# Hybrid decoder trunk: in the state-space mixer, the injection of the next inputs goes behind the state outputs, the direct part and gelu go bank by bank, and GpSimd's input powers wait for other events

## The chip, the cores and the metric

One Trainium2 chip, one core of it. The metric is the device time of one execution in microseconds (us); lower is better. The engines are TensorE (PE in the profile), VectorE (DVE), ScalarE (ACT), GpSimd (POOL) and SyncE (SP), which issues nearly all transfers.

## The reference

A trunk of two layers over 16 meta tokens and 512 tokens of width 1024 (L = 528). Layer 0 mixes with a diagonal state-space model (S5), layer 1 with differential attention; a gated convolutional feed-forward net follows each. All in float32. The part that matters here is the S5 mixer, cut short:

```python
def s5_mixer(u, ...):                      # u: (1, 528, 1024), 64 groups of 16 channels
    bu = einsum('blgc,gnc->blgn', ug, bb)  # complex; 64 states for each group
    s  = scan of s[l] = a_bar * s[l-1] + bu[l]
    y  = re(einsum('blgn,gcn->blgc', s, c)) + d_skip * u
    z  = gelu(y)
    h  = z @ w_glu + b_glu                 # then val * sigmoid(gate)
```

## The kernel before

Each engine runs a program of its own, written out by hand in order; semaphores (`wait_ge`, `then_inc`) tie them together. Nothing schedules: an engine that waits holds up all that stands behind it in its program.

**Blocks and rounds.** The mixer cuts time into 66 blocks of T = 8 steps, and the 1024 channels into CT = 8 tiles of 128 channels (8 groups). The loop `for b in range(CT)` works on one tile in each round. For tile b the output is a direct part inside each block of 8 steps (a Toeplitz matrix `TT`, built from small kernels in `Kp`) plus a part from the state at the block's start. So each tile goes through:

- `x_transposes`, `gather` (ACT), `u_transposes`, `u_out` (ACT): the normalized inputs in the form `U`. Profile lines L684, L1215, L695, L1224.
- `input_power`: products of powers and weights, `F1` and `F2`, two instructions each. For tile 0 on DVE; for tile 1 `F1b` on DVE and `F2b` on POOL; from tile 2 all four instructions on POOL (L551). Then `input_weights` on PE (L709, L711) and `weights_out` on ACT (`WBT`, L1274).
- `inject` on PE (L744): `WBT` times `U` into PSUM banks 2 and 3. It counts `v_ps`.
- `scan` on DVE (L1720 to L1727), which waits for `v_ps`, then `states` (L1734 to L1741). `s_half` is counted when it has read banks 2 and 3 for the last time, `s_set` when the states `Sst` are there.
- `state_outputs` on PE (L764) into banks 6 and 7, then `direct_outputs` (L772), which adds `TT` times `U`, counts `y_ps`, and leads to `gelu` on ACT (L1313).
- `kernel_products` on PE (L728, L733), `kernel_out` on ACT (L1284, counts `k_copied`), and `toeplitz`, eight transfers on SP's queue (L603) which write `TT`; `direct_outputs` waits for them (`tt_in`).
- `z_transposes` (L783), `z_round` (L1321), `z_rests` (L792, L795), `z_low` (L1328): the gelu's output as two fp32r parts, the input of the GLU product (`glu_part`, L818).

On DVE, round b holds `scan(b)`, `states(b)`, and then for tile b+1 `output_product` and `output_powers` (`E`, counts `e_set`), and for tile b+2 the rotation tables (counts `t_set`). On ACT it holds `z_round`, in rounds 1 and 2 one `split_hi` of a GLU weight (L297), `weights_out`, `z_low`, `turn_out`, `u_out`, `gather`, `decay`, `gelu`, `kernel_out`, `mirror`. In the last round PE fills its wait for the states with parts of the first GLU product, whose bank is free once `k_copied` has come to 8.

`u_transposes(b+1)` writes the same banks 2 and 3 as `inject`, so the order on them is `inject(b)`, scan and states, `u_transposes(b+1)`, `u_out(b+1)`, `inject(b+1)`.

Of the kernel before, what the change touches and what calls it, by code (L numbers as in the profile page):

```python
# [33 lines left out]
CT = D // P  # L34
# [106 lines left out]
def build(nc, inp, out):  # L141
# [3 lines left out]
    with ctx:  # L145
# [301 lines left out]
        s_set = sem("s_set")  # L447
        y_ps = sem("y_ps")
        gelu_set = sem("gelu_set")
        zt_ps = sem("zt_ps")  # L450
# [202 lines left out]
        def _(pe):  # L653
# [113 lines left out]
            def direct_outputs(b):  # L767

                pe.wait_ge(tt_in[b % 2], (b // 2 + 1) * T * 16)
                for q in range(BQ):  # L770
                    for e in range(2):
                        mm = nc.tensor.matmul(y_at(q, e), U[:, b % 2, 2 * q + e], TT[:, b % 2, :, 2 * q + e],  # L772
                                              start=False, stop=q == BQ - 1)
                mm.then_inc(y_ps, 1)

# [53 lines left out]
            kernel_products(0)  # L829
            u_transposes(0)  # L830
            for b in range(CT):
                inject(b)
                if b:
# [7 lines left out]
                else:  # L841
                    glu_part(0, 0, 3)
                    z_rests(b - 1)
                    glu_part(0, 3, CT - 2)
                state_outputs(b)
                direct_outputs(b)
                if b + 1 < CT:
# [338 lines left out]
        def _(act):  # L1186
# [120 lines left out]
            def gelu(b):  # L1307
                act.wait_ge(y_ps, b + 1)
                if b:
                    act.wait_ge(zr_ps, b)  # L1310
                for h in range(2):
                    o = Z2[:, :, :].rearrange("k j (q e c) -> k e q j c", q=BQ, e=2)[:, h]
                    ins = nc.scalar.activation(  # L1313
                        o, ps[0:NK, 6 + h, :].rearrange("k (q j c) -> k q j c", q=BQ, j=T), ACT.Gelu_apprx_tanh)
                ins.then_inc(gelu_set, 1)
# [652 lines left out]
        def _(pool):  # L1968
# [41 lines left out]
            V.memset(tp[0][:, 0:1], 0.0).then_inc(ta_set, 1)  # L2010
            pool.wait_ge(v_ps, 1)
            input_power(V, F2b, P2, Bsw, 1).then_inc(f_set, 1)
            for b in range(2, CT):
                pool.wait_ge(v_ps, b - 1)
                pool.wait_ge(ft_ps, b - 1)
                input_power(V, F1[b % 2], P1, Bst, b)
                input_power(V, F2[b % 2], P2, Bsw, b).then_inc(f_set, 1)
            for n in range(2):
                pool.wait_ge(v_ps, CT - 1 + n)
                split_lo(pool, n, n)  # L2020
# [105 lines left out]
```

## Time and profile before

| | |
|---|---|
| Median of 3 runs | 1275.64 us (1275.29 to 1275.65) |
| The profiled execution | 1275.05 us, span 1273.0 us |
| Busy share of the span | PE 98%, PEld 93%, DVE 59%, ACT 45%, POOL 48% |
| 46 to 117 us (six rounds), busy of 71 us | PE 68.77, DVE 65.03, ACT 63.36, POOL 23.96 |
| From 120 us on | PE busy in every slice; GLU, feed-forward, attention, feed-forward |

The span is the time from the first to the last recorded instruction; 2.05 us lie around it. The mixer's rounds take from about 33 us to about 128 us. Only there and in the prologue before it does the change move anything.

### The profile page before, as it was taken

What the parts mean: (1) busy time and instruction counts of PE and PEld (TensorE: products, weight loads), DVE (VectorE), ACT (ScalarE), POOL (GpSimd) and SP (SyncE); (2) the same over time, 40 slices, a digit from 0 to 9 for tenths busy, and PEclk for the clock granted to TensorE, in tenths of its full rate; (3) what the DMA queues carried; (4) which work ended last, traced back from release to release, by engine and by line L of the source; (5) the groups of instructions that cost most, each with busy time, mean ns of one, the idle gap of its engine ahead of it and who ended that gap; (6) DMA issues with size and microseconds to landing.
All of it is one profiled execution on the core that took longest, in us unless ns stands there. A gap on an engine that the chain in (4) does not pass through costs nothing.

```text
span 1273.0 us, 26292 instructions
## 1 busy us (share of the span) xinstructions
PE 1243.4 (98%) x10335; PEld 1185.3 (93%) x10335; DVE 751.6 (59%) x1028; ACT 570.7 (45%) x957; POOL 607.4 (48%) x361
## 2 busy tenths in 40 slices
PE   5899999999999999999999999999999999999998
PEld 5888999999999999999998988989999999998886
DVE  8997122688888884111455555553688888882002
ACT  7996543343343432222656656633243333432113
POOL 5433566444444345656654544419544344444431
PEclk9999999999999999999999999999999999999999
DMA  8333332223322333333222112113323333233231
GB/s 174 67 72 82 102 100 84 75 75 99 99 82 87 95 95 91 93 91 112 70 69 65 50 51 68 34 50 100 97 71 97 99 96 86 82 99 99 99 99 66
DMA packets 179498, 108.88 MB, mean 86 GB/s; under 512 B 7100, under 2 KB 173789, under 8 KB 179165
## 3 DMA queue, kind: packets, MB, share of 16 engines
q1 hardware_dynamic: 178997, 107.31, 30.0%
q8 instruction: 51, 0.84, 0.3%
q10 hardware_dynamic: 432, 0.59, 0.1%
q14 instruction: 18, 0.15, 0.0%
HBM read 101.59 MB, written 2.10 MB: 81 GB/s over the span
## 4 chain that ended last, share of the span: by engine, by line
PE 86%; issue 6%; POOL 4%; DVE 2%; ACT 1%; DMA 0%; SPq 0%; POOLq 0%; DVEq 0%; ACTq 0%
PE ps L314 49%; PE ps L987 10%; PE ps L937 10%; PE ps L818 7%; PE ps L1024 2%; PE ps L1094 2%; PE ps L772 1%; POOL acc L2028 1%; PE ps L764 1%; PE ps L1070 1%; POOL sqt L2027 1%; PE ps L1028 0%; PE ps L744 0%; DVE ps L1727 0%; PE ps L711 0%
## 5 line engine op out<-in xcount | busy, mean ns | idle before, releaser
L301 POOL TENSOR_TENSOR wL<-raw,wH 128x1024 fp32r<-128x1024 f32 x182 | 446.9, 2467 | 548.8 <-ACT wH L297 523.0
L314 PE MATMUL ps<-hgH,wH 128*128 128x264 f32 (+1 forms) x1408 | 285.3, 284 | 0.0
L314 PE MATMUL ps<-hgH,wL 128*128 128x264 f32 (+1 forms) x1408 | 285.3, 284 | 0.0
L314 PE MATMUL ps<-hgL,wH 128*128 128x264 f32 (+1 forms) x1408 | 285.0, 284 | 0.0
L297 ACT ACTIVATE wH<-raw 128x1024 fp32r<-128x1024 f32 x182 | 186.4, 1048 | 216.4 <-PE ps L314 79.0
L314 PEld LDWEIGHTS ps<-hgH,wH 128*128 128x128 f32 x1408 | 218.9, 189 | 0.1
L314 PEld LDWEIGHTS ps<-hgL,wH 128*128 128x128 f32 x1408 | 218.4, 189 | 0.0
L314 PEld LDWEIGHTS ps<-hgH,wL 128*128 128x128 f32 x1408 | 217.8, 189 | 0.0
L1402 ACT ACTIVATE cg<-cg 128x528 f32<-128x528 f32 (+1 forms) x44 | 28.2, 640 | 266.7 <-DVE cg L1807 266.7
L1807 DVE SCALAR_TENSOR_TENSOR cg<-u,PV,cg 128x528 f32<-128x528 f32 (+1 forms) x88 | 104.9, 1192 | 13.0 <-DVE cv L1801 6.7
L1801 DVE TENSOR_SCALAR cv<-u,PV 128x528 f32<-128x528 f32 (+1 forms) x44 | 111.3, 2530 | 0.0
L987 PE MATMUL ps<-hgH,wH 128*128 128x264 f32 x384 | 83.2, 298 | 0.0
L987 PE MATMUL ps<-hgH,wL 128*128 128x264 f32 x384 | 78.2, 285 | 0.0
L987 PE MATMUL ps<-hgL,wH 128*128 128x264 f32 x384 | 77.9, 284 | 0.0
L314 PE MATMUL ps<-actH,wL 128*128 128x264 f32 x352 | 71.2, 283 | 0.0
L314 PE MATMUL ps<-actH,wH 128*128 128x264 f32 x352 | 71.2, 283 | 0.0
L314 PE MATMUL ps<-actL,wH 128*128 128x264 f32 x352 | 71.2, 283 | 0.0
L1807 DVE SCALAR_TENSOR_TENSOR cv<-u,PV,cv 128x528 f32<-128x528 f32 (+1 forms) x88 | 66.2, 752 | 0.0
L1829 DVE TENSOR_TENSOR ytok<-ps,fgain 128x512 f32<-128x512 f32 x4 | 2.8, 692 | 103.2 <-ACT ysq L1421 103.2
L1465 ACT ACTIVATE Pb<-ps,tiny 128x144 f32<-128x144 f32 (+4 forms) x66 | 34.8, 532 | 63.2 <-DVE tiny L1855 63.1
L987 PEld LDWEIGHTS ps<-hgH,wH 128*128 128x128 f32 x384 | 59.3, 189 | 3.9 <-issue 3.8
L1763 DVE SCALAR_TENSOR_TENSOR hgL<-hT,PV,hgH (+1 forms) x24 | 34.9, 1455 | 43.2 <-ACT hgH L1373 43.2
(301 smaller groups left out, 2384.8 us busy)
## 6 DMA issues: line engine op xcount, KB each, us to landing
raw<-ffn_w_up SPq DMA_DIRECT2D x88, 512.0 KB, 3.8
raw<-ffn_w_down SPq DMA_DIRECT2D x38, 512.0 KB, 3.6
raw<-attn_w_qkv SPq DMA_DIRECT2D x24, 512.0 KB, 3.7
raw<-s_w_glu SPq DMA_DIRECT2D x16, 512.0 KB, 4.0
TT<-KD SPq DMA_DIRECT2D x64, 64.0 KB, 2.4
raw<-attn_w_o SPq DMA_DIRECT2D x8, 512.0 KB, 4.1
raw<-ffn_w_down SPq DMA_DIRECT2D x8, 384.0 KB, 3.4
xb<-x SPq DMA_DIRECT2D x8, 256.0 KB
```

The lines of the kernel that those rows point to most:

```text
L297: nc.scalar.activation(wH[:, slot, 0:nk], raw[:, slot % 2, 0:nk], ACT.Copy).then_inc(w_hi, 1)
L301: nc.gpsimd.tensor_tensor(wL[:, slot, 0:nk], raw[:, slot % 2, 0:nk], wH[:, slot, 0:nk].bitcast(F32), ALU.subtract).then_inc(w_lo, 1)
L314: mm = nc.tensor.matmul(ps[:, bank + b, 0:tw], w[:, slot, k0 + k, :], x[:, kt, t0:t0 + tw], start=first and k == 0 and s0, stop=last and k ...
L818: mm = nc.tensor.matmul(ps[:, bank + b, 0:tw], w[:, n % 4, k, :], x[:, k, t0:t0 + tw], start=k == 0 and s0, stop=k == 7 and s1)
L937: mm = nc.tensor.matmul(ps[:, 2 * t + c, :], x[:, kt, tok], w[:, n % 4, 4 * c:4 * c + 4], start=False, stop=last and w is ws[-1] and x is ...
L987: mm = nc.tensor.matmul(ps[:, unit_bank(n) + b, 0:tw], w[:, n % 4, k, :], x[:, k, t0:t0 + tw], start=k == 0 and s0, stop=k == 7 and s1)
L1024: return nc.tensor.matmul(ps_row[:, base[c] + a:base[c] + b], q[half[c], q0:nk], k[half[c], a:b], start=True, stop=stop)
L1402: nc.scalar.activation(cg[:, t0:], cg[:, t0:], ACT.Silu).then_inc(silu_set[l], 1)
L1465: ins = nc.scalar.activation(Pb[:, c, 0:nk], score_row(i, c), ACT.Exp, bias=mn[:, c:c + 1], scale=-1.0, accum_out=esum[:, c:c + 1])
L1763: V.scalar_tensor_tensor(hgL[:, ds(ct, 1)], hT[:, ds(ct, 1)], PV[:, ds(gain, 1)], hgH[:, ds(ct, 1)].bitcast(F32), ALU.mult, ALU.subtract). ...
L1801: ins = V.tensor_scalar(c[k][:, t0:], u[:, k, 2 + t0:2 + L], col(i, CONV_W + (3 * l + 2) * 2 * FT + k * FT + q), col(i, CONV_B + l * 2 * F ...
L1807: ins = V.scalar_tensor_tensor(c[k][:, t0:], u[:, k, t0 + j:L + j], col(i, CONV_W + (3 * l + j) * 2 * FT + k * FT + q), c[k][:, t0:], ALU. ...
```

## The change

On PE, `inject(b+1)` is issued between `state_outputs(b)` and `direct_outputs(b)`. Before, it stood behind `direct_outputs(b)` and `kernel_products(b+1)`, at the head of round b+1. `direct_outputs` does bank 6 first and then bank 7, and counts a semaphore after each (`y_half`, `y_ps`); `gelu` does its first half after the first. On POOL, `F2b` waits for `f1_set` (DVE has finished `F1b`) in place of `v_ps`; the powers of tile b wait for `t_set` (DVE's rotation tables of tile b-1) besides; the first two `split_lo` wait for `t_set` and `e_set` in place of `v_ps`.

```diff
@@ def direct_outputs(b)
-                for q in range(BQ):
-                    for e in range(2):
+                for e in range(2):
+                    for q in range(BQ):
                         mm = nc.tensor.matmul(y_at(q, e), U[:, b % 2, 2 * q + e], TT[:, b % 2, :, 2 * q + e],
                                               start=False, stop=q == BQ - 1)
-                mm.then_inc(y_ps, 1)
+                    mm.then_inc((y_half, y_ps)[e], 1)
@@ PE's rounds
+            inject(0)
             for b in range(CT):
-                inject(b)
...
                 state_outputs(b)
+                if b + 1 < CT:
+                    inject(b + 1)
                 direct_outputs(b)
                 if b + 1 < CT:
                     kernel_products(b + 1)
@@ def gelu(b)
-                act.wait_ge(y_ps, b + 1)
                 if b:
                     act.wait_ge(zr_ps, b)
                 for h in range(2):
+                    act.wait_ge((y_half, y_ps)[h], b + 1)
@@ POOL
-            pool.wait_ge(v_ps, 1)
+            pool.wait_ge(f1_set, 1)
             input_power(V, F2b, P2, Bsw, 1).then_inc(f_set, 1)
             for b in range(2, CT):
                 pool.wait_ge(v_ps, b - 1)
+                pool.wait_ge(t_set, b)
                 pool.wait_ge(ft_ps, b - 1)
...
             for n in range(2):
-                pool.wait_ge(v_ps, CT - 1 + n)
+                if n == 0:
+                    pool.wait_ge(t_set, CT)
+                else:
+                    pool.wait_ge(e_set, CT)
                 split_lo(pool, n, n)
```

How the order on the engines moves. First PE, from the state outputs of round 6 to the first GLU product of round 7 (each other round has the same piece, with the input weights in the GLU product's place). `ps<-U,WBT` is the injection, `ps<-TT,U` the direct part, `ps<-E,Bst` and `ps<-dd,cst` the kernel products. Before:

```order
L764 MATMUL ps<-E,Sst 66x128 [waits wbt_set,s_set]
L764 MATMUL ps<-E,Sst 66x128 x15
L772 MATMUL ps<-TT,U 66x128 [waits tt_in0]
L772 MATMUL ps<-TT,U 66x128 x7
L728 MATMUL ps<-E,Bst 16x128 [waits k_copied,xt_out,e_set]
L728 MATMUL ps<-E,Bst 16x128 x15
L733 MATMUL ps<-dd,cst 16x16 x8
L744 MATMUL ps<-U,WBT 64x66 [waits u_set,wbt_set]
L744 MATMUL ps<-U,WBT 64x66 x15
L783 MATMUL ps<-cst,Z_91 128x66 [waits z_lo,gelu_set]
L783 MATMUL ps<-cst,Z_91 128x66 x7
L818 MATMUL ps<-actH,wH 128x264 [waits k_copied,z_lo,w_lo,w_hi]
```

The same piece of the changed kernel, whose line numbers are one higher:

```order
L765 MATMUL ps<-E,Sst 66x128 [waits wbt_set,s_set]
L765 MATMUL ps<-E,Sst 66x128 x15
L745 MATMUL ps<-U,WBT 64x66 [waits u_set,wbt_set]
L745 MATMUL ps<-U,WBT 64x66 x15
L773 MATMUL ps<-TT,U 66x128 [waits tt_in0]
L773 MATMUL ps<-TT,U 66x128 x7
L729 MATMUL ps<-E,Bst 16x128 [waits k_copied,xt_out,e_set]
L729 MATMUL ps<-E,Bst 16x128 x15
L734 MATMUL ps<-dd,cst 16x16 x8
L784 MATMUL ps<-cst,Z_91 128x66 [waits z_lo,gelu_set]
L784 MATMUL ps<-cst,Z_91 128x66 x7
L819 MATMUL ps<-actH,wH 128x264 [waits k_copied,z_lo,w_lo,w_hi]
```

The sixteen matmuls of the injection have moved ahead of the direct part and the kernel products, with their wait for `u_set`; nothing stands between the kernel products and the transposes that wait for the gelu.

Then POOL at the start of the rounds, where it makes the second powers of tile 1 and those of tile 2. Before:

```order
L2010 MEMSET tmpP 128x1 [waits pool_seq]
L551 TENSOR_TENSOR F2b<-P_119,Bsw 128x4x128 [waits v_ps]
L551 TENSOR_TENSOR F2b<-P_119,Bsw 128x4x128
L551 TENSOR_TENSOR F1a<-P_118,Bst 128x4x128 [waits ft_ps,v_ps]
L551 TENSOR_TENSOR F1a<-P_118,Bst 128x4x128
```

And of the changed kernel:

```order
L2013 MEMSET tmpP 128x1 [waits pool_seq]
L552 TENSOR_TENSOR F2b<-P_119,Bsw 128x4x128 [waits f1_set]
L552 TENSOR_TENSOR F2b<-P_119,Bsw 128x4x128
L552 TENSOR_TENSOR F1a<-P_118,Bst 128x4x128 [waits ft_ps,t_set,v_ps]
L552 TENSOR_TENSOR F1a<-P_118,Bst 128x4x128
```

Here nothing has moved; only the events differ that the instructions wait for.

## Rows read from the trace of the kernel before

**Rows 1.** The page: its first line.

```profile
span 1273.0 us, 26292 instructions
```

**Rows 2.** Chain that ended last, one round: start us, us, what.

```profile
82.38 1.11 PE ps L744 x32
...
83.57 0.70 DVE rt L1720
...
87.70 0.70 DVE rt L1735
...
88.54 0.69 PE ps L695 x8
...
89.25 1.97 PE ps L764 x32
91.21 1.89 PE ps L772 x16
93.11 0.59 PE ps L728 x32
...
93.91 1.11 PE ps L744 x32
```

**Rows 3.** Timeline of PE: start us, us, then what [idle before <-releaser].

```profile
41.23 0.66 PE L684 MATMUL ps<-cst,xb 66*128 66x66 f32 x8
...
41.73 0.66 PE L695 MATMUL ps<-cst,xg 66*128 66x66 f32 x8
...
42.66 1.97 PE L764 MATMUL ps<-E,Sst 64*66 64x128 f32 x32 [0.27 <-ACT WBT L1274]
...
64.06 0.68 PE L684 MATMUL ps<-cst,xb 66*128 66x66 f32 x8
65.02 0.68 PE L695 MATMUL ps<-cst,xg 66*128 66x66 f32 x8 [0.28 <-DVE rt L1735]
```

**Rows 4.** Timeline of DVE: the scans of rounds 1 and 2.

```profile
48.50 0.70 DVE L1720 TENSOR_TENSOR rt<-T,ps 128x528 f32<-128x528 f32 x1 [1.06 <-PE ps L744]
...
60.05 0.71 DVE L1720 TENSOR_TENSOR rt<-T,ps 128x528 f32<-128x528 f32 x1 [0.35 <-PE ps L744]
```

**Rows 5.** Waits, 35 to 135 us: us in total, times, longest us.

```profile
POOL F1b L551 <- PE ps L744: 21.7, 3, 7.2
...
DVE rt L1720 <- PE ps L744: 5.3, 7, 2.1
...
PE ps L709 <- POOL F2b L551: 2.8, 1, 2.8
...
PE ps L772 <- DMA TT<-KD: 0.4, 1, 0.4
```

**Rows 6.** Timeline of ACT in round 2.

```profile
59.07 1.52 ACT L1284 ACTIVATE KD<-ps 16x256 f32<-16x256 f32 x4
...
61.96 1.07 ACT L297 ACTIVATE wH<-raw 128x1024 fp32r<-128x1024 f32 x1
63.29 1.09 ACT L1274 ACTIVATE WBT<-ps 128x512 f32<-128x512 f32 x2 [0.25 <-PE ps L711]
...
66.19 0.71 ACT L1224 ACTIVATE U<-ps 128x264 f32<-128x264 f32 x2
```

**Rows 7.** Timeline of SP's queue, and landing of the TT transfers.

```profile
60.62 4.99 SPq L603 DMA_DIRECT2D TT<-KD  x8
...
72.15 5.65 SPq L603 DMA_DIRECT2D TT<-KD  x8
...
DMA to landing us min/median/max: 2.2/2.4/2.7
```

**Rows 8.** Tile F1b: duration ns min/median/max, first and last start us.

```profile
L551 DVE TENSOR_TENSOR F1b<-P,Bst x2: 691/1140/1590, 33.8 to 34.4; 128x512 f32<-128x512 f32 x2
L551 POOL TENSOR_TENSOR F1b<-P,Bst x2: 1110/1111/1112, 48.5 to 49.6; 128x512 f32<-128x512 f32 x2
```

**Rows 9.** Timeline of POOL at the start of round 0.

```profile
34.30 2.68 POOL L551 TENSOR_TENSOR F2b<-P,Bsw 128x512 f32<-128x512 f32 x2 [4.29 <-PE ps L744]
```

**Rows 10.** Windows: us, busy of PE, PEld, DVE, ACT, POOL, PEclk, DMA, GB/s.

```profile
36.74:40.15 3.41, 3.11 (x15) 3.12 (x16) 3.31 (x7) 3.39 (x12) 3.41 (x5) 0.50 0.61 105
```

**Rows 11.** Timeline at the end of the rounds, PE and ACT.

```profile
117.17 1.52 ACT L1284 ACTIVATE KD<-ps 16x256 f32<-16x256 f32 x4
...
117.98 0.72 PE L783 MATMUL ps<-cst,Z 66*128 66x66 f32 x8
...
118.95 0.48 PE L818 MATMUL ps<-actH,wH 128*128 128x264 f32 x2 [0.25 <-ACT KD L1284]
```

More of the change, by code:

```diff
@@ L448, in build @@
         y_ps = sem("y_ps")
+        y_half = sem("y_half")
         gelu_set = sem("gelu_set")
```

## The prediction, made before the changed kernel ran

> **What bounds the kernel now.** I began with the size of the whole. The span is 1273.0 us [rows 1], and the changed lines run only in the mixer's rounds, seven of about 11.5 us and a last one; behind them PE is busy without a gap, so what PE gains or loses by the first GLU product is what the program gains or loses. Then the chain that ended last, over one round [rows 2]. The reader should see that it goes round once: injection starts 82.38, DVE's scan starts 83.57 (1.19 later), the states have read their banks at 87.70 + 0.70 = 88.40 (4.83), PE's input transposes start 88.54 (0.14), state outputs 89.25 (0.71), direct part 91.21 (1.96), kernel products 93.11 (1.90), next injection 93.91 (0.80). The sum is 11.53 us, the round. The injection stands at the very end of that ring, behind 2.70 us of direct part and kernel products which the scan has no need of. That is what the change attacks.
>
> But the ring is not much longer than the other things a round must do. PE waits in two places: before L695, which starts 65.02 although the eight transposes ahead of it started 64.06 and need only 0.50 when nothing holds them (41.23 to 41.73) [rows 3], so 0.46; and before the state outputs, where 0.71 are spent on 0.50 of transposes [rows 2, 3], so 0.21. PE needs 11.53 - 0.67 = 10.86. DVE waits 0.35 before the scan of round 2, and 1.06 before that of round 1, ahead of which PE had begun late [rows 4]. All such waits are 5.3 us in seven rounds, 2.1 of it in the last [rows 5]; the 2.1 that are left for the other five fit 0.35 in a plain round and more in one with a late transfer. So DVE needs 11.53 - 0.35 = 11.2 us for a round. A round cannot go below 11.20 for long, whatever the order on PE.
>
> **The change part by part.**
>
> *Injection ahead.* Same matmuls, none added. The ring of rows 2 without its 2.70 us, but with the injection's own time, is 8.8 us and binds nothing any more. What binds in its place is the longest of the rings that go through the direct part, since this now comes 1.1 us later behind the state outputs:
>
> 1. The transfer ring. Direct part 1.90, kernel products 0.80 [rows 2], hand-over to ACT about 0.11 (taken near the 0.14 from DVE to PE in the same rows), kernel_out 1.52 and 0.03 until SP issues (59.07 + 1.52 = 60.59, issue 60.62) [rows 6, 7], seven of eight issues 4.99 x 7/8 = 4.37, landing 2.4 [rows 7], hand-over 0.1: 11.2 us. This ring exists today and is hidden by 0.3 us. In one round the eight issues took 5.65 instead of 4.99 us, and PE waited 0.4 us for it [rows 5, 7].
> 2. The ACT ring. Injection 1.1, direct part 1.90, kernel products 0.80, hand-over 0.11, then ACT from kernel_out at 59.07 to the end of u_out at 66.19 + 0.71 = 66.90, less the 0.25 it waited: 7.58 [rows 6]; hand-over to PE 0.1, and the next injection, which waits for `u_set`. The sum is 11.6 us. It is this long in rounds 1 and 2 alone, where ACT has the weight split of 1.07 (L297) between; in the others it is 10.5. Today the injection's wait for `u_set` is covered by the direct part and the kernel products, 2.7 us; the change takes this cover away. What is late there next is the injection, then the direct part behind it.
> 3. DVE's own 11.20.
>
> So I take rounds 1 and 2 at 11.6 (today 11.53): +0.14. The other four at 11.2: 4 x -0.33 = -1.3. The 0.4 us for the late transfer: I count half of it as gone, -0.2, because the transfer has 0.3 us less to be late by but the ring it sits in is the new bound. Together -1.4.
>
> *Gelu by halves.* Today the kernel_out follows the gelu at once. The transposes of the gelu's output lose the injection that stood before them (1.1 us) and keep the kernel products, 0.80; the second gelu half (one of two, about 0.5) starts when the direct part ends, so it ends 0.6 to 0.8 behind it. It fits, with nothing over: 0 taken, and +0.1 a round if not. Had gelu stayed whole, it would have cost some 0.3 to 0.4 a round here. The new order inside the direct part changes no count and no size: 0.
>
> *F2b on POOL.* PE waits 2.8 us for it [rows 5], and it moves the wrong way: today it starts 34.30 and ends 36.98 [rows 9]; now it waits for F1b on DVE. Of DVE's two F1b instructions one took 0.69 and the one under POOL's 1.59; POOL's own, alone, take 1.11 each [rows 8]. Undisturbed, DVE ends at about 34.4 + 0.69 = 35.1, and POOL runs 35.2 to 37.4. That is 0.4 late. PE then runs at half of its 2.4 GHz: the granted clock is 0.50 from 36.74 to 40.15 [rows 10]. Work that starts 0.4 later inside that stretch has 0.4 us less of the slow clock to run in, so half is given back: +0.2. DVE starts its first scan about 0.6 earlier, and it had idled 1.1 in front of the second. That makes DVE the engine that is ahead, and is worth nothing by itself.
>
> The same rows are what the Trainium skill describes (SBUF — State Buffer, section "SBUF: two separate sides"): VectorE instructions with two SBUF inputs and GpSimd's hold the shared pair of ports one at a time, for a whole instruction. The trace agrees there, 1.59 against 0.69. By that rule the shifted POOL instructions would now hold up DVE's sums of the first states, two of them behind 1.11 us each; the states, ready near 41.0 without it (35.2, the 4.83 of rows 2 and an estimate of 1.0 for the two sums), would be there at 43.2 at the worst, where PE, at 42.66 today [rows 3] and 0.2 later, wants them at about 42.9. The sum would be +0.3 us more.
>
> *Later powers and weight splits.* `t_set` for tile b comes directly ahead of the scan on DVE, which is when POOL starts today, and the powers take four times 1.11 us of a round with 7.2 us of idle before them [rows 5, 8]: 0. The second split_lo may go 2 us earlier; its user, the second GLU unit, stands behind all of round 7: 0.
>
> *The end of the rounds.* In round 7 the transposes of the gelu (117.98) are followed by the GLU product (118.95), which waits for kernel_out (117.17 + 1.52 = 118.69, so 0.26 of hand-over) [rows 11]. Today the injection lies between kernel products and transposes and covers that copy. Now the transposes come straight behind the kernel products, and the GLU product 0.11 + 1.52 + 0.26 = 1.89 us behind them instead of 0.97: +0.9. The states of round 7, 2 us earlier, help nobody: PE goes from the GLU parts to the state outputs without a gap already.
>
> **Sum.** +0.2 - 1.4 + 0.9 = -0.3 us; with the whole of the late transfer gone -0.5, and I take -0.4. The profiled execution took 1275.05 (its span and 2.05 around it), 0.6 under the median, so -0.4 is put on the median 1275.64: 1275.2 us. A measurement of this kernel can tell about 0.2% (2.5 us) from no change; this is a sixth of it.
>
> **The rivals.**
>
> *Everything fits* (0.12). Landing at 2.2 and a gapless ACT: all six rounds at DVE's 11.20, -2.0, the transfer's 0.4 gone too, start +0.2, end +0.9: -1.3 us, 1274.3. If the copy at the end were also covered, -2.2, 1273.4. Against it: rounds 1 and 2, where ACT's own instructions add up past that.
>
> *The change doesn't act* (0.10). The wait only changes its name, from DVE waiting for `v_ps` to PE waiting for `u_set` or `tt_in`, at 11.5 in every round: 0, and start and end remain: +1.1 us, 1276.7. For it: two rings within 0.1 us of today's round.
>
> *A second stretch at half clock* (0.06). PE idles from 34.2 to 37.4, not to 37.0, ahead of the slow stretch [rows 10]. If the clock stayed down for as long again, 3.4 us at half cost up to 1.7 us, less what PE waits anyway: +1.2, 1276.4.
>
> *Slower beyond doubt* (0.02). The issues of all rounds take 5.65 us, as in one round now [rows 7]. The ring is then 11.2 + 0.58 = 11.8, six rounds +1.6, with start and end +2.7, 1278.3. It decides from some 0.6 us of delay in every round; one of seven shows it.
>
> The likeliest, -0.9 to +0.3, has 0.70.
>
> **How the numbers follow.** The range goes to the covered copy below (-2.0, 1273.6) and to the rival without effect and a little late transfer above (+1.2, 1276.8). Faster by over 0.2% needs more than all the waits of the rounds: 0.03. Slower by over 0.2%: 0.02. Within: 0.95.
>
> **What would show it.** DVE's wait before the scan gone from the list, PE's before L695 as well; new ones, PE at the injection for ACT's `U` in rounds 1 and 2 (0.3 or more each in three places), PE at L772 for the transfer in the others, and about 1 us at the first GLU product for `KD`. Round lengths, injection to injection: 11.6, 11.6, then 11.1 to 11.3. F2b's two instructions at 1.11 each, ended near 37.4. DVE idle before a scan would prove me wrong on what binds; rounds under 11.15 on what DVE needs. A difference beyond 2 us would have to come from a place that the diff doesn't touch.

## The result, and the profile after

1277.6 us (median of 19 runs, 1276.4 to 1278.6) against 1275.5 of the kernel before on the same chip (20 runs, 1274.9 to 1276.1): ratio 1.0017, interval 1.0011 to 1.0023. One more run of the changed kernel (1439.8 us) and one of e2 below (1728.5 us) ran at a granted clock of 0.80 and 0.66 in the mean and are left out. The changed kernel is slower by 2.1 us: under the 0.2% that the prediction set as the least that can be told, but the interval leaves out 1, and the time lies above the range of 1273.6 to 1276.8. The page and the waits of the changed kernel, 35 to 140 us, against [rows 1, 5]:

```profile
span 1276.0 us, 26292 instructions
```

```profile
POOL F1b L552 <- DVE T L1702: 21.3, 3, 7.6
...
DVE rt L1723 <- ACT R L1299: 3.7, 6, 1.1
...
PE ps L710 <- POOL F2b L552: 3.4, 1, 3.4
PE ps L773 <- DMA TT<-KD: 2.6, 4, 1.1
...
PE ps L819 <- ACT KD L1287: 1.2, 1, 1.2
```

DVE hardly waits for the injection any more. In its place PE waits for the transfers, 2.6 us instead of 0.4. The chain that ended last, one round, against [rows 2] (start us, us, what):

```profile
79.56 2.27 DMA TT<-KD
...
81.87 1.96 PE ps L773 x16
83.83 0.58 PE ps L729 x32
84.42 0.28 PE ps L734 x16
...
84.72 0.38 ACT KD L1287
...
86.28 0.56 SPq L604
...
90.68 3.44 DMA TT<-KD
...
94.17 1.85 PE ps L773 x15
```

This is the transfer ring of the prediction, now the bound. (A ring is a chain of waits that comes back to its start one round later; the longest one sets the length of a round.) But from 81.87 to 94.17 it takes 12.30 us, not 11.2: the last transfer runs 3.44 us from the start of its issue, where the one before ran 2.27. SP's queue and the spread of the landings, against [rows 7]:

```profile
62.62 4.97 SPq L604 DMA_DIRECT2D TT<-KD  x8
...
74.70 5.39 SPq L604 DMA_DIRECT2D TT<-KD  x8
...
86.28 6.12 SPq L604 DMA_DIRECT2D TT<-KD  x8
```

```profile
L604 SPq DMA_DIRECT2D TT<-KD x56: 507/589/1721, 51.1 to 127.0; - x56
...
DMA to landing us min/median/max: 2.2/2.4/3.4
```

A single issue takes up to 1.72 us (the 1721 ns of this line) instead of 0.59. And the end of the rounds and the windows, against [rows 11] and [rows 10]:

```profile
119.96 0.71 PE L784 MATMUL ps<-cst,Z 66*128 66x66 f32 x8
121.90 0.48 PE L819 MATMUL ps<-actH,wH 128*128 128x264 f32 x2 [1.24 <-ACT KD L1287]
```

```profile
36.01:42.83 6.82, 5.78 (x30) 5.78 (x31) 6.65 (x11) 5.00 (x15) 5.44 (x5) 0.50 0.38 67
```

The first GLU product starts 121.90 - 118.95 = 2.95 us later; the span is 3.0 longer. From here on times inside a profile are counted from the first injection (32.53, before 33.06), since the prologue ahead of it ends anywhere between 32.4 and 34.2 us in the profiles. So counted, the loss is 89.37 - 85.89 = 3.48 us.

A table serves for all that follows: the rounds, from the first matmul of one direct part to that of the next, out of PE's timelines.

| kernel | tile 0 to 1 | 1-2 | 2-3 | 3-4 | 4-5 | 5-6 |
|---|---|---|---|---|---|---|
| before | 11.55 | 11.52 | 12.00 | 11.52 | 11.53 | 11.53 |
| changed | 11.53 | 12.08 | 11.58 | 12.30 | 11.28 | 11.81 |
| before, half the transfers (e6) | 11.52 | 11.52 | 11.52 | 11.52 | 11.52 | 11.53 |
| changed, half the transfers (e5) | 11.52 | 11.54 | 11.13 | 11.14 | 11.13 | 11.12 |
| before, filler on PE (e8) | 11.56 | 12.22 | 11.58 | 12.52 | 11.52 | 12.55 |
| before, 16 transposes (e11) | 11.52 | 12.37 | 11.59 | 12.13 | 11.52 | 12.85 |
| before, 80 transposes (e12) | 12.43 | 11.52 | 12.43 | 11.52 | 12.32 | 11.53 |
| changed, 64 transposes (e13) | 12.24 | 11.52 | 12.31 | 11.21 | 12.25 | 11.23 |
| before, 16 transposes, half the transfers (e15) | 11.56 | 11.52 | 11.52 | 11.52 | 11.52 | 11.52 |
| kernel products first (e20) | 12.05 | 12.45 | 12.43 | 12.46 | 12.45 | 12.45 |

### The profile page after: what moved, and what is told of

It is laid out like the page before. It is cut to its first block, busy times and chain, and to the rows that moved or that the text cites. A ratio compares the mean times of both kernels' runs of the same rounds, so it can differ in the third digit from the quotient of the medians.

```text
span 1276.0 us, 26292 instructions
## 1 busy us (share of the span) xinstructions
PE 1244.3 (98%) x10335; PEld 1186.1 (93%) x10335; DVE 751.5 (59%) x1028; ACT 572.4 (45%) x957; POOL 606.9 (48%) x361
## 4 chain that ended last, share of the span: by engine, by line
PE 85%; issue 5%; POOL 4%; SPq 2%; ACT 2%; DMA 1%; DVE 1%; POOLq 0%; DVEq 0%; ACTq 0%
PE ps L314 49%; PE ps L990 10%; PE ps L940 10%; PE ps L819 7%; PE ps L1027 2%; SPq L604 2%; PE ps L1097 2%; PE ps L773 1%; DMA TT<-KD 1%; POOL acc L2035 1%; ACT KD L1287 1%; PE ps L1073 1%; POOL sqt L2034 1%; PE ps L1031 0%; PE ps L729 0%
```

## The experiments

Medians stand beside the median of the kernel before on the same chip.

### First: which part of the change, which place

**e1, PE and ACT alone:** the changed kernel with POOL's waits as before.

```diff
-            pool.wait_ge(f1_set, 1)
+            pool.wait_ge(v_ps, 1)
...
-                pool.wait_ge(t_set, b)
```

> PE's and ACT's part of the change alone (injection ahead, direct part and gelu bank by bank), with GpSimd waiting as before. Theory A (the loss of 2.2 us is made of three pieces: about 1 us at the start, where GpSimd's new wait makes PE idle longer and a stretch at half clock lasts 6.8 us in place of 3.4; about 0 to 1 us in the rounds, where the ring of direct part, kernel products, kernel_out and TT transfers is the bound; 1.0 us at the end, where the GLU product waits for kernel_out): the start piece goes, so about 1.0 to 1.5 us less than the changed kernel, 1276.2 to 1276.7, and the slow stretch in the trace is 3.4 us. Rival B (it is all in the rounds and the end, the clock is chance): as the changed kernel, 1277.7. Both: GpSimd starts its powers earlier, under VectorE's E instructions, which lengthens some of these; if that reaches PE the time is above 1277.7.

Measured 1285.8 us (before 1275.8), ratio 1.008, interval 1.0066 to 1.0094: missed by far. The injection now ends early, so `v_ps` lets POOL begin 3.7 us ahead of the scan (58.26 against 61.94), while DVE works on its rotation tables:

```profile
58.26 2.31 POOL L552 TENSOR_TENSOR F1a<-P,Bst 128x512 f32<-128x512 f32 x2 [6.99 <-PE ps L745]
...
61.94 0.70 DVE L1723 TENSOR_TENSOR rt<-T,ps 128x528 f32<-128x528 f32 x1
```

DVE's groups, 50 to 110 us (x, busy us, mean ns), first of e1 and then of the changed kernel:

```profile
L1700 DVE TENSOR_TENSOR tmpE<-TAB 128x160 f32<-128x160 f32 x4 | 3.8, 954 | 0.1
```

```profile
L1700 DVE TENSOR_TENSOR tmpE<-TAB 128x160 f32<-128x160 f32 x5 | 1.6, 324 | 0.2
```

324 ns became 954, and a round up to 14.6 us long (from scan to scan, 75.82 to 90.46). PE then waits, and its granted clock falls to 0.50 twice more than in the changed kernel, for 3.4 us from 66.86 and 6.8 us from 94.17. So the later start of POOL's powers, by `t_set`, which I had costed at 0, is what makes the moved injection bearable. (The other waits of POOL went back too; their share was not measured apart.)

**e2, POOL alone:** the kernel before with the new waits of POOL.

```diff
-            pool.wait_ge(v_ps, 1)
+            pool.wait_ge(f1_set, 1)
...
+                pool.wait_ge(t_set, b)
```

> GpSimd's new waits alone, PE and ACT as before. Theory A: the rounds and the end stay as they were (round 11.53 us), the start loses 1.0 to 1.5 us by the longer stretch at half clock: 1276.5 to 1277.0. Rival B: 1275.5 within 0.3, with the slow stretch at 3.4 us.

Measured 1276.3 us (median of 10 runs; before 1275.8), ratio 1.0003, interval 0.9993 to 1.0012. Two runs lie at 1275.5 and 1275.6, the others from 1276.1 to 1276.8. By itself no difference can be told.

**e3, the last injection back** behind the kernel products, the others ahead.

```diff
-                if b + 1 < CT:
+                if b + 1 < CT - 1:
                     inject(b + 1)
...
+                if b == CT - 2:
+                    inject(CT - 1)
```

> The changed kernel, but the injection for the last tile stands behind the kernel products again. Theory A: the wait of 1.2 us before the first GLU product falls to 0.25 and the time by 0.9 to 1.0, to about 1276.8. Rival C (the end piece is hidden, for what the GLU product waits less the later transfer takes): no change from 1277.7, and the direct part of the last round waits for its transfer instead.

Measured 1277.9 us (1275.8), ratio 1.0018, interval 1.0009 to 1.0027: no gain. PE at the end of its rounds:

```profile
115.69 1.96 PE L773 MATMUL ps<-TT,U 128*66 128x128 f32 x16 [1.75 <-DMA TT<-KD]
...
120.33 0.48 PE L819 MATMUL ps<-actH,wH 128*128 128x264 f32 x2
```

The wait for `KD` at the GLU product is gone, and 1.75 us at the direct part of tile 6 have taken its place. From there to the GLU product it is 4.64 us, as in the changed kernel (121.90 - 117.26) and nearly as before (118.95 - 114.20 = 4.75). Here the wait at the end was no loss of its own: the transfers decide. Where they don't, in e19 below, the last injection's place is worth 1.1 us.

**e4, PE kept busy:** the changed kernel with work on PE in the gap ahead of the slow stretch.

```diff
             inject(0)
+            for _ in range(22):
+                nc.tensor.transpose(ps[:, 1, 384:512], ident, ident)
```

> The changed kernel with 22 transposes of the identity into an unused part of bank 1 behind the first injection, so that PE is busy while it waits for F2b; their result isn't used. Theory A: no stretch at half clock near 36 us, input_weights(1) takes 2.7 us in place of 5.4 us, and the time falls by 1.5 to 2.5 us, to 1275.2 to 1276.2. Rival B (the half clock is covered by what ACT has to do at that point): no change beyond 0.3 us.

Measured 1277.0 us (1275.8), ratio 1.0009, interval 1.0 to 1.0018, the runs spread from 1275.0 to 1278.3. That is some 0.9 us of the 2.1 back, less than theory A's 1.5 to 2.5. No stretch at half clock is left, yet PE still waits for late transfers, 1.4 us in all.

**e10, the first moved injection back:**

```diff
-                if b + 1 < CT:
+                if 0 < b < CT - 1:
                     inject(b + 1)
...
+                if b == 0:
+                    inject(1)
```

> The changed kernel with the injection of tile 1 alone put back behind the direct part of tile 0 and the kernel products of tile 1; all others stay ahead. Theory A (the ring of the transfers starts with the first direct part, so the 1.1 us of injection put in front of it are lost for good and the later rounds can't win them back): the direct part of tile 0 starts 1.1 us earlier, the GLU product 0.8 to 1.1 us earlier, 1276.7 us. Rival (DVE or ScalarE sets the pace from tile 1 on): the later scan of tile 1 pushes the rest back, no gain, 1277.7 us.

Measured 1277.4 us (1275.3), ratio 1.0019, interval 1.001 to 1.0028: no gain. The direct part of tile 0 came 1.18 us earlier (12.97 behind the first injection, not 14.15), and the next round took 12.60 us, since DVE now waited for the injection. The rival was right; theory A falls on this point.

```profile
50.30 0.70 DVE L1725 TENSOR_TENSOR rt<-T,ps 128x528 f32<-128x528 f32 x1 [2.24 <-PE ps L745]
```

### Second: are the transfers the bound?

**e5 and e6, half the transfers,** in the changed kernel and in the kernel before (the waits count accordingly):

```diff
-                for i in range(T):
+                for i in range(0, T, 1 if b < 2 else 2):
```

> The changed kernel with every second of the eight Toeplitz transfers left out from tile 2 on (half of the matrix TT keeps the values of an earlier tile, so the output is not the reference's; all matmuls stay). The ring direct part, kernel products, kernel_out, issues, landing gets some 2.5 us shorter (four issues of 0.62 us less). Theory A (the changed kernel's rounds are bound by this ring, and each late issue or landing now shows in full): the wait of PE at the direct part for the transfer goes, rounds come to 11.6, 11.6 and then 11.2 to 11.3 us, together 2 to 2.5 us less than in the changed kernel: about 1275.3 us. Rival B (the rounds are bound by the ring through ScalarE, u_out and the injection in front of the direct part): at most 0.5 us less, rounds still 11.5 to 12.3, about 1277.3 us. Rival C (the long rounds come from DVE): no change at all and the wait ahead of the scan stays.

> The kernel before with the same four of eight transfers left out from tile 2 on (half of TT is stale, the output is not the reference's). Theory A: in this kernel the transfer ring is hidden behind the injection ring of 11.53 us, so only the late ones show: 0.4 to 0.6 us less than the kernel before, about 1275.1 us, rounds of 11.53 throughout. Rival B: the transfers disturb other engines or the fetch of instructions in both kernels; then it gains as much here as in the changed kernel, 2 us or more.

Measured 1274.9 and 1274.8 us (1275.3; both ratios 0.9997, interval 0.9988 to 1.0006). Each against the kernel before on its own chip, the changed kernel goes from 2.1 us above it to 0.4 below, 2.5 us in all, and the kernel before gets 0.5. In both kernels the rounds are those of the prediction (table). So the loss goes through the transfers; with half of them gone the two kernels can't be told apart.

**e8, the filler of e4 in the kernel before.**

> The kernel before with 22 transposes of the identity into an unused part of a bank behind the first injection, where PE would idle for 2.8 us. Theory A (the stretch at half clock that follows this idle time costs PE real work in the kernel before too): no stretch at half clock, direct part of tile 0 about 1 us earlier, first GLU product about 1 us earlier, 1274.5 us. Rival (the first round of the kernel before waits for DVE, not for PE): the stretch goes but the first GLU product comes at the same time, 1275.6 us.

Measured 1277.7 us (1275.3), ratio 1.0018, interval 1.0009 to 1.0027. Neither theory: without any stretch at half clock it is 2.4 us slower, as slow as the changed kernel. Three transfers were late, by up to 1 us. That led to the next step. It also bears on the comparison itself: with this filler in both, the changed order is no longer behind, 1.2 us above the kernel before (e4) against 2.4 (e8), and 86.40 against 87.89 us from the first injection to the GLU product.

### Third: what makes a transfer late

The DMA view of the changed kernel, from the last issue of tile 2 on (66.97 to 69.90), and in the second fence the same for tile 3 (79.46 to 82.00). The columns of a queue are packets, MB, share of 16 engines; those of TT are issues, KB each, us to landing.

```profile
q1 hardware_dynamic: 121, 0.21, 40.5%
q8 instruction: 1, 0.02, 2.9%
...
TT<-KD SPq DMA_DIRECT2D x1, 64.0 KB, 3.2
```

```profile
q1 hardware_dynamic: 101, 0.16, 33.6%
q14 instruction: 2, 0.02, 1.8%
...
TT<-KD SPq DMA_DIRECT2D x1, 64.0 KB, 2.3
```

Queue 8 carries packets of 16 KB with instructions, 51 in the span, each some 1 us long (0.88 to 1.55 in the rounds of this trace). One such packet lies in the landing that took 3.2 us, none in that of 2.3. It is the same in all traces in which SP alone issues, 128 landings: in the 17 in which such a packet began 0.5 to 1.3 us behind the start of the last issue, the last data packet ended 1.75 to 2.41 us behind the end of that issue; in the other 111 it ended 1.35 to 1.47 us behind. And of 928 issues all 25 that took more than 0.95 us had such a packet open.

Whose are they? In the rounds one comes for about 120 matmuls and as many weight loads of PE (108 to 136 between two packets in the changed kernel, 84 to 176 in the kernel before; both average 123 to 124). In the kernel before there are three stretches without any, 255 to 485, 539 to 618 and 931 to 1161 us, with 1878, 649 and 1848 matmuls. PE's compare-and-branch records lie in just these three: there it runs loops, and code that repeats needs no new packet. The Trainium skill says the same (Advanced Engine Details and Errata, section "ISA Cache"): TensorE's code comes in lines of 16 KB, 256 instructions; the trace agrees, some 246 and the waits between. And why one packet on one of sixteen engines holds up all: the Trainium skill (DMA: Bandwidth & Descriptors, section "Queues, rings and completion order") has a semaphore's increment land only behind all earlier writes of that DMA engine, whatever the queue. The late landings fit that. Which DMA engine carried which packet, no trace here tells, so this last link is argued and not shown.

If so, PE's instruction count decides which transfer is hit. **e11, e12, e13:** small transposes on PE at 18.5 to 24.8 us, where it idles; 16 and 80 in the kernel before, 64 in the changed one.

```diff
             x_transposes(0)
+            for _ in range(16):
+                nc.tensor.transpose(ps[0:GC, 6, 384:384 + GC], ident[0:GC, 0:GC], ident[0:GC, 0:GC])
             input_weights(0)
```

> The kernel before with 16 small transposes (16 by 16, into a free corner of bank 6) on PE between 18.5 and 24.8 us, where PE idles; nothing else changes. The traces show packets of 16 KB with instructions, about 1 us long on one DMA engine, one for about 120 matmuls and as many weight loads of PE. In the kernel before they fall 1.8 to 2.4 us behind the last issue of a tile (landed by then) or at the first issue; in the kernel with the filler behind the first injection they fell 1.2 us behind the last issue of three tiles, and those transfers landed 0.6 to 0.8 us later. Theory A (PE's program, fetched over the same DMA engines, delays the transfers, and where it falls depends on the count of PE's instructions): with 16 more pairs the packets fall 0.4 to 1.0 us earlier, 5.4 to 5.9 us behind the first issue, into the landing: three transfers late, PE waits for the transfer 1.5 to 2.5 us in all, 1276.5 to 1277.8 us. Rival (coincidence; the filler's 2.4 us had another cause, such as the clock): no change, 1275.4 us.

> The same with 80 small transposes. Theory A: counted from the trace of the kernel before, the packets of three rounds now fall between 0.7 us ahead of the first issue and that issue, the others past the landing: hardly a late transfer, 1275.0 to 1275.5 us, less than with 16 although PE does more. Rival (the added work itself costs): slower than with 16 transposes. Second rival (no effect of PE's count): the same as the kernel before and as with 16.

> The changed kernel with 64 such transposes. Theory A: the packets move by some 0.6 us to the issues' later part in the even rounds (4.4 us behind the first issue) and to its very start in the others; the ring has no slack, so every hit costs: three hits as before, 1276.5 to 1278 us, with other rounds long than in the changed kernel. Rival (no effect of PE's count): the long rounds stay 2, 4 and 6.

Measured 1279.0, 1278.4 and 1276.9 us (1275.4); ratios 1.0028 (1.0017 to 1.0039), 1.0021 (1.0012 to 1.003), 1.0012 (1.0003 to 1.0021). Sixteen transposes in idle time cost 3.5 us, more than the change, where 1.1 to 2.4 had been expected. Tile 2 of e11, where PE starts its direct part, and the DMA view of that landing (64.76 to 67.70):

```profile
68.24 1.96 PE L772 MATMUL ps<-TT,U 128*66 128x128 f32 x16 [0.77 <-DMA TT<-KD]
```

```profile
q8 instruction: 1, 0.02, 2.0%
...
TT<-KD SPq DMA_DIRECT2D x1, 64.0 KB, 3.4
```

The packet began 1.27 us behind the last issue's start, 5.6 us behind the first; 5.4 to 5.9 had been forecast. Tiles 2, 4 and 6 are late. With 80 the forecast missed: the packets fell 0.8 to 1.3 us behind the last issue's start of tiles 1, 3 and 5. I had counted the shift from the undisturbed rounds, but each late transfer moves all later packets against the rounds. With 64 in the changed kernel the long rounds are the first, third and fifth, not the second, fourth and sixth that the rival asked for. So the count decides which are late, though I can't forecast the time from it. Of the versions that only add instructions to PE, the two of the changed order (e4 and e13) are 1.2 and 1.5 us above the kernel before, and the three of the old order (e8, e11 and e12) 2.4 to 3.5. Their intervals overlap in part, and in the profiles e13 is level with e11 and e12 (88.20, 88.22 and 88.06 us from the first injection to the GLU product). So the changed order isn't shown to be faster there, but the old one's lead is gone.

**e15, the 16 transposes with half the transfers.**

> The kernel before with the 16 small transposes and with every second Toeplitz transfer left out from tile 2 on (half of TT is stale, the output is not the reference's). Theory A (the 16 transposes cost 3.5 us only because they move packets of PE's program onto the landings): with four issues the transfers are there 2.5 us early and a late one is hidden: rounds 11.53 throughout, 1274.9 us, as the half-transfer kernel without the transposes. Rival (they cost by something else, the clock, the prologue, PE's fetch itself): 1.5 to 3.5 us above that, 1276.5 to 1278.5 us.

Measured 1275.3 us (1275.4), ratio 0.9997, interval 0.9988 to 1.0006. The 3.5 us are gone, the rounds are 11.52. Apart from what they do to the transfers, the transposes cost nothing that can be told (0.4 us more than e6, each against its own chip, with intervals that are the same).

### Fourth: can the ring be relieved with all work done?

**e14, the last two transfers of tiles 2 to 7 by POOL,** behind its powers.

```diff
-                for i in range(T):
+                for i in range(T if b < 2 else T - 2):
                     sp.dma_start(TT[i * GC:(i + 1) * GC, b % 2], Kp[:, i:i + T]).then_inc(tt_in[b % 2], 16)
...
+            def last_transfers(b):
+                pool.wait_ge(k_copied, b + 1)
+                for i in range(T - 2, T):
+                    nc.gpsimd.dma_start(TT[i * GC:(i + 1) * GC, b % 2], Kp[:, i:i + T]).then_inc(tt_soft[b % 2], 16)
```

> The changed kernel with the last two of the eight Toeplitz transfers of tiles 2 to 7 issued by POOL, behind its powers, at the same time as SP issues the other six (all work is done, nothing left out). Theory A (the ring through the transfers is the bound): SP's part ends 1.2 us earlier; where POOL is free in time the ring falls under DVE's 11.2 and a packet of 1 us is hidden again: rounds 11.5, 11.5, 11.2, 1275.0 to 1275.8 us. Rival (POOL's transfers cost more to issue and to land than SP's and come behind 4.4 us of powers): the wait of PE at the direct part stays or grows, 1277.5 us or more.

Measured 1291.8 us (1275.4), ratio 1.0134, interval 1.0119 to 1.015. The rival, by another way than it said. POOL's timeline, and on DVE the sum of the states that pays for it, once and as a group:

```profile
78.31 1.03 POOL L2025 DMA_DIRECT2D TT<-KD  x2 [9.89 <-ACT KD L1293]
79.36 2.18 POOL L558 TENSOR_TENSOR F1b<-P,Bst 128x512 f32<-128x512 f32 x2
81.49 2.16 POOL L558 TENSOR_TENSOR F2b<-P,Bsw 128x512 f32<-128x512 f32 x2
```

```profile
79.52 4.43 DVE L1749 TENSOR_TENSOR Sst<-rt,rt 128x260 f32<-128x260 f32 x1
```

```profile
L1749 DVE TENSOR_TENSOR Sst<-rt,rt 128x260 f32<-128x260 f32 x4 | 13.1, 3286 | 0.1
```

POOL waits 9.9 us for `k_copied` with the next powers queued behind, so these run at the same time as DVE's sums of the states: 3286 ns in the mean where the same one takes 429 in the changed kernel, and PE waits 10.7 us for them in all.

**e16 and e17, one transfer by ScalarE,** in the changed kernel and in the kernel before.

```diff
-                for i in range(T):
+                for i in range(T - (b > 2)):
...
+                if b > 2:
+                    act.wait_ge(k_copied, b + 1)
+                    nc.scalar.dma_start(TT[(T - 1) * GC:T * GC, b % 2], Kp[:, T - 1:2 * T - 1]).then_inc(tt_in[b % 2], 16)
```

> The changed kernel with the last of the eight Toeplitz transfers of tiles 3 to 7 issued by ScalarE right behind its kernel_out, while SP issues seven (all work done). Theory A: the ring is 0.6 us shorter in those tiles, a late packet costs 0.6 less each time: rounds 3, 4, 5 and 6 together some 1.2 to 2 us less, 1275.7 to 1276.6 us. Rival (the issue occupies ScalarE for 0.6 us or more and the ring through ScalarE and u_out becomes the bound): no gain or slower, 1277.7 to 1279 us, with PE waiting for ACT's U.

> The same move in the kernel before. Theory A: its ring through the transfers is hidden, so at most the one late transfer is won: 0 to 0.4 us, 1275.1 to 1275.5 us. Rival (the issue on ScalarE delays u_out and gelu): 1276 us or more.

Measured 1281.0 us (ratio 1.0047, interval 1.0033 to 1.006) and 1275.5 us (0.9999, 0.999 to 1.0008) against 1275.4. ScalarE and SP's queue of e16:

```profile
86.67 0.56 ACTq L1294 DMA_DIRECT2D TT<-KD  x1
87.27 0.32 ACT L1309 ACTIVATE T<-T 128x132 f32<-128x132 f32 x1 [0.64 <-ACT KD L1287]
```

```profile
86.66 4.78 SPq L604 DMA_DIRECT2D TT<-KD  x7
```

The issue takes 0.6 us out of ScalarE in each of these rounds, and its ring (10.5 in the prediction) becomes the bound: rounds of 11.8 to 11.9, one of 12.5. (That is 0.7 more than 10.5 and the issue make; ScalarE's own wait for PE at L1334 is 0.4 of it.) The rival had the right ring but the wrong wait. PE waits for ScalarE's `z_round` (2.7 us, four times), and for `U` no longer than in the changed kernel (0.6). Nor does SP win 0.6: one of its seven issues takes 1.03 us with no instruction packet open, so it ends only 0.2 earlier than eight undisturbed ones. The Trainium skill (DMA: Bandwidth & Descriptors, section "Issuing engines are not separate DMA queues") says that all issuers share the same DMA engines; the longer issue fits that, but no run here shows which DMA engines were used.

**e18,** e16 with the filler of e4 and the last injection of e3.

> The changed kernel with the ScalarE issue of e16, the 22 transposes of the identity behind the first injection (no stretch at half clock) and the last injection back behind the kernel products. Theory A: against e16 0.6 to 1.0 us for the clock and 0.5 to 0.9 us at the end, where the direct part of tile 6 no longer waits for its transfer: 1274 to 1275 us, at or below the kernel before. Rival (the packets fall anew and the sum of parts doesn't hold): 1275.5 to 1277 us.

Measured 1277.0 us (1275.4), ratio 1.0014, interval 1.0005 to 1.0023: 4 us below e16, but the rival's range. ScalarE's ring stays at 11.8 a round.

**e19,** e5 with the filler and the last injection back.

> The changed kernel with every second Toeplitz transfer left out from tile 2 on (half of TT is stale, the output is not the reference's), with the 22 transposes of the identity behind the first injection and the last injection back behind the kernel products. Theory A (the sum of the prediction holds where the ring is out of play: rounds 11.5, 11.5 and four at 11.13, no stretch at half clock, nothing lost at the end): 0.5 to 1.5 us less than the 1274.9 us of the kernel before with half the transfers: 1273.4 to 1274.4 us. Rival (the injection's place is worth nothing in any case): 1274.9 us.

Measured 1272.0 us (1275.5), ratio 0.9973, interval 0.9963 to 0.9984, better than expected. From the first injection to the GLU product it is 83.38 us, against 84.98 in e5 and 85.36 in e6. The last injection back gives 1.1 of this: the time from the direct part of tile 5 to that of tile 6 is 10.04 instead of 11.12. The filler gives 0.5 (the first direct part 12.28 behind the first injection, not 12.76); in the old order it gives 0.3 (11.20 in e8, 11.49 before). So by the profiles an order with all but the last injection ahead is worth 85.36 - 83.38 - 0.3 = 1.7 us if nothing waits for transfers. The medians differ by 1 us more, which stays open.

**e20, kernel products first,** so that the transfers start earlier.

```diff
                 if b + 1 < CT:
                     inject(b + 1)
+                    kernel_products(b + 1)
                 direct_outputs(b)
-                if b + 1 < CT:
-                    kernel_products(b + 1)
+                if b + 2 < CT:
+                    x_transposes(b + 2)
...
-                gelu(b)
                 if b + 1 < CT:
                     kernel_out(b + 1)
-                    if b + 2 < CT:
-                        mirror(b + 2)
+                gelu(b)
+                if b + 2 < CT:
+                    mirror(b + 2)
```

> The changed kernel with the kernel products of tile b+1 ahead of the direct part of tile b, kernel_out ahead of the gelu on ScalarE, and the input transposes of tile b+2 behind the direct part to cover the later gelu (all work done). Theory A: the transfers start 1.9 us earlier in the round, so the ring is out of play even with a late packet; but the gelu ends 0.8 to 1.1 us later against PE, of which the transposes cover 0.5: rounds of 11.5 to 11.9 without a wait at the direct part, 1276 to 1278 us. Rival (gelu is covered, rounds at DVE's 11.2): 1274 to 1275 us, below the kernel before.

Measured 1281.0 us (1275.5), ratio 1.0038, interval 1.0024 to 1.0052. The transfers are out of play as theory A has it, but its size missed: no wait for a transfer is left among PE's waits, while rounds are 12.45 us, with DVE and PE waiting for ScalarE:

```profile
DVE rt L1725 <- ACT R L1301: 7.0, 6, 1.3
...
PE ps L784 <- ACT Z L1318: 3.1, 7, 0.9
```

No version with all its work done was faster than the kernel before as it stands.

## Why the prediction was wrong

**The loss in parts,** from the first injection to the GLU product in the profiles. Without late transfers and with equal clocks, e5 against e6: 84.98 - 85.36 = -0.38. The slow clock, 6.8 us instead of 3.4: the first direct part came 14.15 - 12.76 = 1.39 later than in e5. Transfers: 89.37 - 1.39 - 84.98 = 3.0 in the changed kernel, 85.89 - 85.36 = 0.53 before. -0.38 + 1.39 + 3.0 - 0.53 = 3.48. Of the 3.0, some 0.6 is the undisturbed ring (11.28 from tile 4 to 5, against 11.13 in e5, four times), and 2.4 the rounds that came out longer. In the medians the transfers cost 2.5 - 0.5 = 2.0 us of the loss of 2.1.

**The step that failed** is the term for the late transfer: "I count half of it as gone, -0.2, because the transfer has 0.3 us less to be late by but the ring it sits in is the new bound". In place of -0.2 the runs show +2.5 (3.0 - 0.53) in the profiles and +2.0 in the medians. I had named the ring, and that it would be bare. Its undisturbed length was right: 11.2 us forecast, 11.21 to 11.28 in the rounds of the changed kernel and of e13 that nothing disturbs. But I took one late transfer in seven as all that comes. A ring without slack pays every delay in full: the packets meet it in about every second round and cost 0.5 to 1.2 us each (the table, against e5). In the kernel before, in tiles 1 to 6, the packets fell at the first issue or 1.8 us and more behind the last issue's start, where they cost little, and 0.3 us of slack hid most of the rest; I took this for the size of the disturbance. This term takes the median from the 1275.2 predicted to about 1277.4, nearly all of the way to 1277.6. The rival "slower beyond doubt", with 0.58 us in every round and 1278.3 us, was nearest, at a chance of 0.02.

The sign of the difference also has luck in it. The kernel before happens to stand where the packets cost it 0.5 us; each of the three versions that add instructions to it was slower, by 2.4 to 3.5 us, where the two of the changed order (e4 and e13) are 1.2 and 1.5 us above it. A difference of over 2 us, the prediction said, would have to come from a place that the diff doesn't touch. That was half right: the diff touches no transfer and adds no instruction, but it moves the packets against the issues and takes away the slack that had hidden them.

**Rounds, -1.4.** Right where the transfers are out of play: e5 has 11.52, 11.54 and four at 11.13, together 67.58 against 69.13 us in e6, -1.55. From 72 us on, in those four rounds, DVE has no wait before its scans, so it is the floor as forecast; 11.13 is within the forecast 11.1 to 11.3, though a hair under the 11.15 that was to prove the estimate of DVE's need wrong. The other sign of being wrong did come up in the changed kernel: DVE idles before its scan, 3.7 us in six times, for ScalarE's `R`. With the transfers halved 1.2 us are left, all before 72 us, so most of it goes with the late transfers.

**Start +0.2 and end +0.9.** The sum is right, 1.17, the places are not: +1.27 at the first direct part (1.1 of it the injection that now stands ahead) and -0.10 behind the last. The wait of 1.2 us for `KD` is there as forecast, but it only shows the same 1.1 us at the other end, so that the sum came out right partly by luck.

**F2b.** Two instructions in 2.16 us and DVE's two `F1b` at 0.69 each, as forecast. The rule of the shared ports, which the prediction cites from the Trainium skill, shows in one of the two sums of the first states, 1.33 us instead of 0.42 (1.34 in e5). It cost nothing in e5: the states were there at 42.4, and PE began the state outputs at 43.33, when ScalarE's `WBT` came.

**The second stretch at half clock** (0.06) came in the profile, priced at up to 1.7, measured 1.4. The change alone doesn't bring it: with PE's new order it is 3.4 us long in e3, e5 and e13 and 6.8 in e1, e10, e14, e16 and e20; with the old order 3.4 in e6, e11 and e12 and 6.8 in e2, e15 and e17. The mean granted clock of a run tells nearly the same of runs without a profile: with 6.8 us it is 0.997 or less, with 3.4 us 0.998 or more (but 0.997 in e11). By that 17 of 33 runs of the kernel before have the long stretch on the chip of e5, with a median 0.6 us above the others, and 14 of 19 of the changed kernel. Whether the change makes it more frequent, and what decides between the two, stays open.

**Gelu, later powers.** PE waits for no gelu in the changed kernel: 0 was right. The powers' 0 was right for what the change does, though e1 shows what stands behind it: 8 us above the changed kernel.

## What to carry to other kernels

When a change takes the slack from a ring that goes through DMA, size that ring by its late transfers, not by the median: look at every issue and landing in the trace, and at what made the late ones late, even where they cost nothing yet. In a program written out at length, the instruction packets are such a cause, and where they fall changes with every instruction added; so compare two orders at more than one alignment (with a few instructions added in idle time, which shifts the packets) before a difference of 2 or 3 us is put down to the order. Here the order lost 2.1 us as it stood, and its median was 1.2 us the lower one with the same filler in both, though the intervals overlap. Leaving out part of the transfers in both kernels separated the transfers' share from the order's within one run each.

## What was not expected of the hardware

- PE's own code, 16 KB for about 120 matmuls and as many loads, comes by DMA at the same time as the data and delays it: with such a packet open a landing of 2.4 us takes 2.8 to 3.9, an issue of 0.59 up to 1.72 in the changed kernel. 16 tiny transposes in idle time cost 3.5 us that way.
- One transfer issued by ScalarE at the same time as SP issues seven makes one of SP's issues 1.03 us long.
- A DVE sum of 429 ns takes 3286 ns in the mean of four, and 4.43 us once (79.52 to 83.95 in e14), when four of POOL's instructions of 1.1 us run beside it.
- After 2.8 to 3.4 us of idle PE the granted clock is 0.50, 1.2 of 2.4 GHz, for 3.4 or for 6.8 us; with transposes in that gap (e4, e8) it stays at 1.00.
